# Six gate groups beside attention: the sum copies issued by SyncE, scores, transposes and value products at other places

## What is computed

```python
h = rmsnorm(x, attn_norm_g)
z = h @ w_in                                   # u, v, pool input, q, k, v of 4 heads
gates = sigmoid(h @ w_gate + b_gate)           # 1024 x 3072: the six gate groups
y_a = gmlp_mixer(...); y_b = pool_mixer(...)
y_c = diff_attn_mixer(q, k, v, ...)            # per head: two softmaxes, p0 - lam*p1, times v
merged = g_a * (y_a @ proj_a) + g_b * (y_b @ proj_b) + g_c * (y_c @ proj_c)
x = x + merged @ w_out
```

## Time and profile before

| | us |
|---|---|
| median of 3 runs | 1463.52 (1463.35 to 1465.45) |
| the profiled execution, its own time | 1465.08 |
| its span in the profile | 1462.6 |
| PE busy | 1416.9 (97%) |
| DVE busy | 1113.6 (76%) |
| ACT busy | 796.9 (54%) |
| DMA, mean rate | 161 GB/s |

### The profile page before, as it was taken

How to read it: one execution, slowest core, us unless ns; L and a number is a source line. 1 busy time by engine, 2 the same in 40 slices (tenths; PEclk the granted TensorE clock), 3 DMA queues, 4 the chain that set the end, 5 groups by cost and what they waited for, 6 DMA issues and landing times.

```text
span 1462.6 us, 23129 instructions
## 1 busy us (share of the span) xinstructions
PE 1416.9 (97%) x8993; PEld 1259.7 (86%) x8993; DVE 1113.6 (76%) x1613; ACT 796.9 (54%) x1136; POOL 104.0 (7%) x129
## 2 busy tenths in 40 slices
PE   9999696989999999999999999999999999999998
PEld 7878695978889999999988787778888889999896
DVE  4868565567699879969876776877565697978888
ACT  6436464632656556546563555535443865748474
POOL 0111111000000100010000000000000000010100
PEclk9999898999999999999999999999999999999999
DMA  8879887542447766586243233233211768585761
GB/s 302 276 213 264 213 255 195 168 168 87 138 122 218 190 183 173 153 227 154 80 176 116 87 119 111 73 101 101 73 58 58 212 164 231 142 240 149 223 152 72
DMA packets 63974, 235.48 MB, mean 161 GB/s; under 512 B 7256, under 2 KB 7768, under 8 KB 63236
## 3 DMA queue, kind: packets, MB, share of 16 engines
q1 hardware_dynamic: 46752, 167.01, 33.2%
q0 software_dynamic: 12864, 56.11, 19.3%
q10 hardware_dynamic: 4260, 11.00, 2.2%
HBM read 231.96 MB, written 31.23 MB: 180 GB/s over the span
## 4 chain that ended last, share of the span: by engine, by line
PE 82%; DMA 9%; issue 5%; DVE 2%; POOL 1%; ACT 1%; SPq 0%; POOLq 0%; DVEq 0%; ACTq 0%
PE ps L2356 26%; PE ps L2357 25%; PE ps L2358 25%; DMA gate_sums<-gates_dram 6%; DMA gate_sums<-gate_sums 2%; PE ps L4025 1%; POOL gate_sums L2238 1%; PE ps L2520 1%; PE ps L2535 1%; PE ps L3925 1%; POOL gate_sums L2235 0%; PE ps L2408 0%; DMA tables<-tables_dram 0%; DVE y L3718 0%; PE ps L4045 0%
## 5 line engine op out<-in xcount | busy, mean ns | idle before, releaser
L966 ACT ACTIVATE wh<-stage 128x1024 fp32r<-128x1024 f32 x147 | 154.8, 1056 | 236.6 <-PE ps L2358 202.4
L2357 PE MATMUL ps<-hl,wh 128*128 128x256 f32 (+1 forms) x832 | 276.5, 332 | 0.0
L2356 PE MATMUL ps<-hh,wh 128*128 128x512 f32 (+1 forms) x760 | 260.0, 342 | 0.1
L2358 PE MATMUL ps<-hh,wl 128*128 128x512 f32 (+1 forms) x760 | 256.3, 337 | 0.0
L1484 DVE TENSOR_TENSOR wl<-stage,wh 128x1024 fp32r<-128x1024 f32 x146 | 177.7, 1221 | 72.5 <-ACT wh L966 72.4
L2357 PEld LDWEIGHTS ps<-hl,wh 128*128 128x128 f32 x832 | 158.2, 190 | 13.5
L2356 PEld LDWEIGHTS ps<-hh,wh 128*128 128x128 f32 x760 | 144.3, 190 | 17.9 <-issue 2.9
L2358 PEld LDWEIGHTS ps<-hh,wl 128*128 128x128 f32 x760 | 144.3, 190 | 15.5
L3013 ACT ACTIVATE wh<-raw 128x1024 fp32r<-128x1024 f32 x75 | 78.7, 1054 | 50.8 <-PE ps L2358 44.7
L3605 DVE TENSOR_TENSOR wl<-raw,wh 128x1024 fp32r<-128x1024 f32 x75 | 90.9, 1219 | 20.2 <-ACT wh L3013 19.8
L1919 DVE TENSOR_TENSOR wl<-raw,wh 128x1024 fp32r<-128x1024 f32 (+1 forms) x75 | 88.7, 1186 | 22.4 <-ACT wh L1263 21.8
(11 more groups left out here) (519 smaller groups left out, 3812.5 us busy)
## 6 DMA issues: line engine op xcount, KB each, us to landing
stage<-stream_dram SPq DMA_DIRECT2D x110, 512.0 KB, 3.3
raw<-up_dram SPq DMA_DIRECT2D x64, 512.0 KB, 7.1
raw<-down_dram SPq DMA_DIRECT2D x52, 512.0 KB, 6.0
gate_sums<-gates_dram POOLq DMA_DIRECT2D x36, 512.0 KB, 7.7
stage<-gate_sums SPq DMA_DIRECT2D x24, 512.0 KB, 4.1
stage<-gates_dram SPq DMA_DIRECT2D x18, 512.0 KB, 7.0
raw_sum<-up_dram SPq DMA_DIRECT2D x16, 512.0 KB, 3.4
raw_sum<-up_dram POOLq DMA_DIRECT2D x16, 512.0 KB, 8.4
```

Source lines behind the costliest of these rows:

```text
L966: A(parts_of(b, p)[0], b.stage[:, p.stage, :], ACT.Copy).then_inc(s.hi_ready, 1)
L2356: MM(out, wh, xh, start=start, stop=False, skip_group_check=True)
L2357: MM(out, wh, xl, start=False, stop=False, skip_group_check=True)
L2358: return MM(out, wl, xh, start=False, stop=stop, skip_group_check=True)
```

## The change

Plain copies of first blocks (four a group, one for every sum) are issued by SP, between its loads of panels 9 to 17; before the copies of groups 2 and 4 it waits until all copies ordered so far have landed. POOL issues only the adds, eight a pair, in three steps instead of six, each sum having its own base: R4's base is block 3, P6's is block 2, and the sum made before is added to it. On PE the scores go to Q5 and P6, the first two transposes to P2 (item six), the other two to R4, the value products to the first step of the next P1. ACT and DVE change their order with them. In group 5 `ych` and `ycl` are made sooner. No instruction of PE, ACT or DVE is added or removed.

```diff
-SUM_LEVEL = {Q5: 8, P7: 8, P6: 12, R4: 16}
+SUM_LEVEL = {Q5: 4, P7: 4, P6: 6, R4: 8}
+SUM_BASE = {Q5: 0, P6: 2, R4: 3, P7: 1}
@@ sync_program
+    def sum_bases(g):
+        if g % 2 == 0 and g:
+            sp.wait_ge(s.gate_bases.sem, s.gate_bases.at(64 * g))
+        for product, r in SUM_BASE.items():
+            sp.dma_start(dram["gate_sums"][g, GATE_SUM[product]],
+                         dram["gates"][g, r]).then_inc(s.gate_bases.sem, 16)
+
+    bases = {9: 0, 10: 1, 12: 2, 13: 3, 15: 4, 16: 5}
     for row in range(2 * RING, P_GATE):
         load_row(row, row - RING)
+        if row in bases:
+            sum_bases(bases[row])
@@ scalar_program, groups 0 to 3
-        gate_seed(i)
         if i:
             act.wait_ge(s.pv_done, i)
         AR(b.vh[:], b.v[:, :, P * i:P * i + P], ACT.Copy).then_inc(s.v_hi, 1)
+        gate_seed(i)
         hi(Panel(first))
+        exps(i, 0)
+        exps(i, 1)
         gate_copy(i, Q5)
         hi(Panel(first + 1))
...
-        exps(i, 0)
-        exps(i, 1)
+        exps(i, 2)
+        exps(i, 3)
         gate_copy(i, P6)
         hi(Panel(first + 2))
...
-        exps(i, 2)
-        exps(i, 3)
         hi(Panel(first + 3))
         hi(Panel(first + 4))
+        turned(i, (0, 1))
         gate_bank(i, P2)
         hi(Panel(first + 5))
+        turned(i, (2, 3))
         gate_differences(i)
-        turned(i, range(TT))
@@ scalar_program, group 5: the four copies to ych now follow hi(Panel(first + 3))
@@ vector_program, groups 0 to 3
-        lo(Panel(first))
...
         score_pair(i, 0, 0, (b.bias, b.bias))
+        score_pair(i, 1, 0, (b.bias, b.bias))
+        lo(Panel(first))
         lo(Panel(first + 1))
-        score_pair(i, 1, 0, (b.bias, b.bias))
...
-        lo(Panel(first + 2))
         for qb in (2, 3):
             score_pair(i, qb, 0, (b.bias, b.bias))
+        lo(Panel(first + 2))
...
+        blend(i)
         gate_sub(i, Q3)
-        blend(i)
         gate_sub(i, P7)
         lo(Panel(first + 3))
+        turned_rest(i, (0, 1))
         lo(Panel(first + 4))
-        turned_rest(i, (0, 1))
@@ vector_program, group 5
-        gate_lo(5)
         if g == 5:
             for h in range(4):
                 head_rest(h)
+        gate_lo(5)
@@ gpsimd_program
+        pool.wait_ge(s.gate_bases.sem, s.gate_bases.at(128 * pair + 128))
         if pair:
-            summed(16 * pair)
+            summed(8 * pair)
         for g in groups:
-            copied(g, 0, dram["gates"][g, 0])
-            copied(g, 3, dram["gates"][g, 1])
-        summed(16 * pair + 4)
+            added(g, Q5, dram["gates"][g, 1])
+            added(g, P7, dram["gates"][g, 2])
+        summed(8 * pair + 4)
         for g in groups:
-            added(g, 0, 1)
-            added(g, 3, 2)
-        summed(16 * pair + 8)
+            added(g, P6, dram["gate_sums"][g, GATE_SUM[Q5]])
+        summed(8 * pair + 6)
         for g in groups:
-            copied(g, 1, dram["gate_sums"][g, 0])
...
+            added(g, R4, dram["gate_sums"][g, GATE_SUM[P6]])
@@ tensor_program
-            between = {P6: {0: [sc(g, 0), sc(g, 1)]}, Q3: {3: [sc(g, 2), sc(g, 3)]},
-                       R4: {1: [tn(g, 0), tn(g, 1)], 4: [tn(g, 2)], 6: [tn(g, 3)]}}
+            between = {Q5: {4: [head_start(g), sc(g, 0), sc(g, 1)]}, P6: {5: [sc(g, 2), sc(g, 3)]},
+                       P2: {6: [tn(g, 0), tn(g, 1)]}, R4: {2: [tn(g, 2)], 4: [tn(g, 3)]}}
             if g:
-                between[P1] = {4: [pv(g - 1)]}
+                between[P1] = {0: [pv(g - 1)]}
+    def head_start(i):
+        def step():
+            pe.wait_ge(s.qk_ready, i + 1)
+            pe.wait_ge(s.yab_written, 4)
+            if i:
+                pe.wait_ge(s.o_evac, i)
+        return step
```

More of the change, by code:

```diff
@@ L402, in semaphores @@
     s.gate_sums = Counted(s.gate_summed, 0)
+    s.gate_bases = Counted(s.lines_set, 1)
     s.gate_copied = Counted(s.line_copied, 1)
@@ L823, in sync_program @@
         if product in GATE_SUM:
-            sp.wait_ge(s.gate_sums.sem, s.gate_sums.at(256 * (g // 2) + 16 * SUM_LEVEL[product]))
+            sp.wait_ge(s.gate_sums.sem, s.gate_sums.at(128 * (g // 2) + 16 * SUM_LEVEL[product]))
             source = dram["gate_sums"][g, GATE_SUM[product]]
@@ L1199, in scalar_program @@
         hi(Panel(first + 3))
+        if g == 5:
+            for h in range(4):
+                act.wait_ge(s.o_normed, h + 1)
+                A(b.ych[:, h, :], b.o[:, h, :], ACT.Copy, scale=b.subln).then_inc(s.yc_hi, 1)
         if g == 4:
@@ L1206, in scalar_program @@
         gate_differences(g)
-        if g == 5:
-            for h in range(4):
-                act.wait_ge(s.o_normed, h + 1)
-                A(b.ych[:, h, :], b.o[:, h, :], ACT.Copy, scale=b.subln).then_inc(s.yc_hi, 1)
         hi(Panel(first + 6))
@@ L2232, in summed, with added @@
         pool.wait_ge(s.gate_sums.sem, s.gate_sums.at(16 * count))
-    def copied(g, n, source):
-        G.dma_start(dram["gate_sums"][g, n], source).then_inc(s.gate_sums.sem, 16)
-    def added(g, n, r):
-        G.dma_start(dram["gate_sums"][g, n], dram["gates"][g, r], accum_op=ALU.add,
+    def added(g, product, source):
+        G.dma_start(dram["gate_sums"][g, GATE_SUM[product]], source, accum_op=ALU.add,
                     max_dma_last_dim=4 * D).then_inc(s.gate_sums.sem, 16)
@@ L2242, in gpsimd_program @@
         groups = (2 * pair, 2 * pair + 1)
+        pool.wait_ge(s.gate_bases.sem, s.gate_bases.at(128 * pair + 128))
         if pair:
-            summed(16 * pair)
+            summed(8 * pair)
         for g in groups:
-            copied(g, 0, dram["gates"][g, 0])
-            copied(g, 3, dram["gates"][g, 1])
-        summed(16 * pair + 4)
+            added(g, Q5, dram["gates"][g, 1])
+            added(g, P7, dram["gates"][g, 2])
+        summed(8 * pair + 4)
         for g in groups:
-            added(g, 0, 1)
-            added(g, 3, 2)
-        summed(16 * pair + 8)
+            added(g, P6, dram["gate_sums"][g, GATE_SUM[Q5]])
+        summed(8 * pair + 6)
         for g in groups:
-            copied(g, 1, dram["gate_sums"][g, 0])
-        summed(16 * pair + 10)
-        for g in groups:
-            added(g, 1, 2)
-        summed(16 * pair + 12)
-        for g in groups:
-            copied(g, 2, dram["gate_sums"][g, 1])
-        summed(16 * pair + 14)
-        for g in groups:
-            added(g, 2, 3)
+            added(g, R4, dram["gate_sums"][g, GATE_SUM[P6]])
     pool.wait_ge(s.omean_ready, 1)
@@ L2615, in tensor_program @@
         for product in ORDER1:
-            if g < 4 and product == P6:
-                pe.wait_ge(s.qk_ready, g + 1)
-                pe.wait_ge(s.yab_written, 4)
-                if g:
-                    pe.wait_ge(s.o_evac, g)
             gate_item(g, product, between.get(product, {}))
```

2 lines of the change are left out of this document (1 added, 1 removed).

## The result

The changed kernel takes 1452.04 us (median of 4 runs, 1451.60 to 1454.93), the kernel before, on the same chip, 1464.49 (4 runs, 1463.35 to 1466.41). The ratio is 0.9916, 95% interval 0.9902 to 0.9930: faster, but above the range of 1424 to 1450. The profiled execution took 1451.6, its span is 1449.5, which is 13.1 less than the span before.

A forecast was written before the change was run, and what follows sets the result against it. PE, busy 97%, was taken to lose time to waits in the gate stage, chiefly late sums. Gains of 27.8 and 6.0 less 2.0 and 3 make 28.8 us: 1463.5 becomes 1434.7, rounded 1435, range 1424 to 1450.

The forecast's parts named there:

- The chain of sums: POOL's sums: a pair shrinks from 71.5 to about 49 us, so both late P6 sums, groups 2 and 4, go.
- The length of a group: Gate stage: 28.6 us a group, bound by DVE and ACT taking turns; groups 1 to 3 gain 27.8 us.
- PE's content: PE's own work in a gate group: 20.1 us for seven items plus 6.2 for the head, given as 26.1.
- rival C: Gate stage: PE's content bounds the group at 26.1 us, giving 1425 us; chance 12%.
- Group 0 and the end of group 5: Gate stage: group 0 loses 2.0 us; earlier `ych` and `ycl` at group 5's end gain 6.0.
- The copies on SP: Ahead of the gate stage: copies between panel loads make P6's sum of group 0 0 to 8 us late; 3 taken.
- the fast rate: DMA from 54 us to P6's sum of group 0: 17.4 MB at 347 GB/s, 50 us; the other rate was 306.
- The deadlines of 92 and 104: Before the gate stage: panel 16 must land by 92 us and panel 17 by 104.
- A: Rival, jammed loads: copies hold up panels 13 to 17 and adds starve; 8 to 20 us more, 1443 to 1455; 15%.
- D: Rival: adds, not copies, cost the time on POOL, so P6's sums stay late; middle 1446 us; 8%.
- B: Rival, slower than before: copies on SP's queue go no faster than pair 0's adds did, delaying panel 17; 1486 us; 5%.
- E: Rival, no difference: bytes ahead of the last sums are the same, sums come when they came; 1460 to 1464 us; 3%.

The follow-up runs named there:

- the bias tile sooner: Kernel after, with ACT asking for the next head's bias tile once this head's score pairs are read, not at the top of the next group: 1449.63 us.
- late lots: Kernel after, with SP issuing pair 1's base copies behind panels 17 and 18 and pair 2's behind 25 and 26: 1445.75 us.
- both edits of ACT: P6's copy and R4's hi ahead of exponentials 2 and 3, next bias tile asked for sooner; added to the kernel after with copies behind 9, 10, 17, 18, 25, 26: 1435.97 us.
- the copies spread: Kernel after with those ACT changes, pair 1's copies two by two behind panels 19 to 22, pair 2's one by one behind 29 to 36: 1424.25 us.

## Why the prediction missed

**The chain of sums: right.** Both late sums went. The 49 us a pair was right for pair 1 (45.3). For pair 0 it was wrong by 28 us (76.9): I took the pace of a pair alone on the DMA engines for one that shares them with 24 copies and nine panels.

**The length of a group: right to 0.1 us.** 28.6 was forecast, 28.57 and 28.64 measured. The waits inside are the ones worked out: `diag` ahead of P7 1.0 (1.3 forecast), the transposes for `s` 0.6 (0.9), for `tl` 0.52 (0.8). With the bias tile sooner, groups 1 to 3 are 85.80 us, the 85.8 of the forecast. PE's content has a slip of 0.2: 20.1 and 6.2 make 26.3, not 26.1. With late lots and both edits of ACT a group is 26.92 with a wait of 0.52 in it, so 26.4. The forecast didn't rest on it, rival C did.

**What the group lacked: the bias tile, 4.0 us.** I moved the score pairs sooner and counted their predecessors on PE, ACT and DVE, but not the transfer of 256 KB they read. Its request stayed at the top of the group, and the time by which the pairs had come later was its cover: 8.4 to 9.3 us from request to first use became 5.2 to 6.6, for a tile that took up to 9.5.

**Group 0 and the end of group 5: right in the sum.** -1.4 for -2.0, and 6.2 for 6.0. In group 0 the parts were not: P7 waited 2.16 us for `diag`, not 4.5, and the transposes 1.71 for `s` and 0.52 for `tl`, not 0.5. That these errors nearly cancel is luck.

**The copies on SP: the step that failed.** It read "So 0 to 8 us late, and I take **3**, nearer the fast rate, since most of the bytes are copies." Measured were 15.5. The bytes were about right: 17.4 MB from 54, and 8.0 (26 us at 308 GB/s), 7.1 (20 us at 353) and 2.9 MB (12 us at 239) make 17.9 by 112. The rate was not the fast one: 17.9 MB in 58 us are 309 GB/s, the slower of my two. P6's sum was asked for at 113.5, 10.5 late, just past the end of that range. Three things were wrong. "The last lot of copies need not, and that is 6 us": the sum didn't need it, but pair 2's two lots stood in the queue ahead of panels 16 and 17 and took their share; their eight copies were 14.3 of the 15.5 us. The deadlines of 92 and 104 for these panels stood in the same paragraph, and I never set them against the queue. Panel 17's was wrong as well: from DVE's start on it to P1 of group 0 is 16.4 us (111.25 to 127.66), and ACT's `hi` takes 1.1 before, so for a start at 112.17 it had to be there by about 95, not 104. And there were several walls close together: with panel 17 out of the way it was panel 18, 1.6 us further on.

**Rivals.** A, the jammed loads, is what came: "It costs 8 to 20 us more than I take", and it cost 12.5 more. The mark I set for it, PE standing still for over 8 us between 85 and 115, showed only 5.7 there; the other 7.8 stood at 127. It had 15%. Against it I had only said that landings overlap, and gave no row for it. C, groups of 26.1, was nearly reached only with both edits of ACT (26.9), and its time of 1425 only with the copies spread as well (1424.25). D's slow adds did show in pair 0, whose first four took 43.9 us (52.57 to 96.49), but the sums of pairs 1 and 2 came in time. B and E did not come.
